# The opening of a two-layer hybrid backbone: order of the first loads, conditioning rows spread by TensorE, and narrow products of 128 columns

## What is computed

```
m_lat = silu(c)     @ ada_w[0] + ada_b[0]        # 9 x 1024 numbers: shift, scale, gate of three sub-layers
m_ctx = silu(c_ctx) @ ada_w[0] + ada_b[0]
h     = rms_norm(x, g) * (1 + scale) + shift     # the context tokens use m_ctx, the latent ones m_lat
x     = x + 0.5 * gate * (silu(h @ W_g) * (h @ W_u)) @ W_out
```

## Time and profile before

| | us |
|---|---|
| median of 3 runs | 2028.41 |
| lowest and highest of them | 2027.28, 2032.01 |
| the profiled execution | 2026.99 |
| its span | 2025.2 |
| PE busy in it | 1984.8 (98%) |
| DVE busy | 1282.0 (63%) |
| ACT busy | 752.2 (37%) |

### The profile page before, as it was taken

How to read it: one execution, slowest core, us unless ns; L and a number is a source line. 1 busy time by engine, 2 the same in 40 slices (tenths; PEclk the granted TensorE clock), 3 DMA queues, 4 the chain that set the end, 5 groups by cost and what they waited for, 6 DMA issues and landing times.

```text
span 2025.2 us, 27640 instructions
## 1 busy us (share of the span) xinstructions
PE 1984.8 (98%) x10255; PEld 1684.6 (83%) x10255; DVE 1282.0 (63%) x1840; ACT 752.2 (37%) x990; POOL 109.3 (5%) x165
## 2 busy tenths in 40 slices
PE   9999999999999999999999999999999999989998
PEld 7888888896788889888888988888887888878886
DVE  6877577775648776877677743453345632656666
ACT  5322222345545334332222342212235432736453
POOL 1010010000003200100001000000000000000000
PEclk8999999999999999999999999999999999999999
DMA  8455455521210003555555532352234422044553
GB/s 351 167 192 180 167 197 167 197 94 42 86 71 21 1 18 108 198 186 174 180 191 170 171 122 98 99 177 103 63 126 149 152 95 104 22 161 141 177 188 123
DMA packets 52650, 274.80 MB, mean 136 GB/s; under 512 B 6128, under 2 KB 7472, under 8 KB 34256
## 3 DMA queue, kind: packets, MB, share of 16 engines
q1 hardware_dynamic: 33024, 203.97, 29.1%
q0 software_dynamic: 18960, 68.88, 10.3%
q10 hardware_dynamic: 576, 0.69, 0.1%
HBM read 272.47 MB, written 1.05 MB: 135 GB/s over the span
## 4 chain that ended last, share of the span: by engine, by line
PE 92%; DVE 4%; ACT 3%; issue 1%; DMA 0%; DVEq 0%; ACTq 0%; SPq 0%
PE ps L1025 15%; PE ps L1027 15%; PE ps L1026 15%; PE ps L1037 8%; PE ps L1255 6%; PE ps L1256 6%; PE ps L1257 6%; PE ps L1038 4%; PE ps L2402 2%; PE ps L2404 2%; PE ps L2403 2%; PE ps L1907 1%; PE ps L1919 1%; PE ps L2488 1%; PE ps L1915 1%
## 5 line engine op out<-in xcount | busy, mean ns | idle before, releaser
L684 DVE TENSOR_TENSOR w_lo<-w_raw,w_hi 128x2048 fp32r<-128x2048 f32 (+3 forms) x206 | 420.8, 2043 | 194.3 <-ACT w_hi L463 193.8
L1025 PE MATMUL ps<-h_parts,w_lo 128*128 128x512 f32 (+1 forms) x1424 | 536.9, 377 | 1.5 <-DVE w_lo L684 0.6
L1027 PE MATMUL ps<-h_parts,w_hi 128*128 128x512 f32 (+1 forms) x1424 | 534.3, 375 | 0.0
L1026 PE MATMUL ps<-h_parts,w_hi 128*128 128x512 f32 (+1 forms) x1424 | 534.2, 375 | 0.0
L463 ACT ACTIVATE w_hi<-w_raw 128x2048 fp32r<-128x2048 f32 (+3 forms) x207 | 353.9, 1710 | 441.4 <-PE ps L1257 254.0
L692 DVE SCALAR_TENSOR_TENSOR ada_product<-ada_w,silu_c 128x1024 bf16<-128x1024 f32 x256 | 313.2, 1223 | 21.1 <-DVE ada_product L692 10.3
L1025 PEld LDWEIGHTS ps<-h_parts,w_lo 128*128 128x128 f32 x1424 | 268.4, 188 | 51.1 <-DVE h_parts L2240 1.1
L1027 PEld LDWEIGHTS ps<-h_parts,w_hi 128*128 128x128 f32 x1424 | 268.3, 188 | 48.5
L1026 PEld LDWEIGHTS ps<-h_parts,w_hi 128*128 128x128 f32 x1424 | 268.4, 189 | 47.5
L475 ACT ACTIVATE sil<-ps 128x512 f32<-128x512 f32 x66 | 39.5, 598 | 481.1 <-PE ps L1027 481.1
L1255 PE MATMUL ps<-hid_parts,w_lo 128*128 128x512 f32 x468 | 182.1, 389 | 0.0
(11 more groups left out here) (337 smaller groups left out, 2545.4 us busy)
## 6 DMA issues: line engine op xcount, KB each, us to landing
w_raw<-in_w_up SPq DMA_DIRECT2D x88, 1024.0 KB, 4.8
ada_w<-in_ada POOLq DMA_DIRECT2D x128, 512.0 KB, 3.6
w_raw<-in_w_down SPq DMA_DIRECT2D x32, 768.0 KB, 4.2
w_raw<-in_w_down SPq DMA_DIRECT2D x32, 640.0 KB, 3.9
w_raw<-in_w_ret_t SPq DMA_DIRECT2D x16, 1024.0 KB, 4.8
w_raw<-in_w_ab SPq DMA_DIRECT2D x14, 1024.0 KB, 4.8
ada<-in_ada SPq DMA_DIRECT2D x8, 1024.0 KB, 21.9
w_raw<-in_w_ret SPq DMA_DIRECT2D x8, 1024.0 KB, 4.8
```

Source lines behind the costliest of these rows:

```text
L684: dve.tensor_tensor(w_lo[parts_of(s, slot)][:, 0:elems], w_raw[slot][:, 0:elems], w_hi[parts_of(s, slot)][:, 0:elems].bitcast(F32), ALU.su ...
L1025: pe.matmul(out, lo, rhs_hi(k), start=first and k == 0, stop=False)
L1026: pe.matmul(out, hi, rhs_lo(k), start=False, stop=False)
L1027: mm = pe.matmul(out, hi, rhs_hi(k), start=False, stop=last and k == nk - 1)
```

## The change

Loads: `ada00[0]` is issued ahead of x. The two broadcast loads of the conditioning rows are gone from SP; ACT now issues them first of all its loads, as two rows of 1024 numbers into partition 0. ACT's order changes: Silu of `c_cols` and of the one-partition rows comes first, then the squares, then the table of the root. PE spreads the rows over the partitions with four products of one row by 512 columns, between the sums of squares; DVE copies the context half out of PSUM and ACT the latent half. The narrow products stream 128 columns (the pair of conditioning columns 64 times over) in place of 2. Both narrow products of chunk 0 run ahead of the sums, chunk 1 also gets its shift from a narrow product (TURNED = 2), and DVE's order of the first chunks is another. Of 49 dummy products in all, 18 stay.

```diff
     def sp_program(sp):
         sp.dma_start(c_cols, a["c_cols"]).then_inc(c_cols_loaded, 16)
+        scale_and_shift(0)
         for i in range(KD // 2):
             sp.dma_start(x[:, 2 * i:2 * i + 2], a["xT"][:, 2 * i:2 * i + 2]).then_inc(x_loaded[i], 16)
         weights(0)
-        scale_and_shift(0)
-        sp.dma_start(silu_c[:, 0, :], a["c_ctx"].partition_broadcast(P)).then_inc(c_loaded, 16)
-        sp.dma_start(silu_c[:, 1, :], a["c"][0, :].partition_broadcast(P)).then_inc(c_loaded, 16)
         scale_and_shift(1)
...
     def scalar_program(act):
+        for st, row in enumerate((a["c_ctx"].unsqueeze(0), a["c"])):
+            act.dma_start(silu_c[0:1, st, :], row).then_inc(c_loaded, 16)
...
-        act.wait_ge(sem("eps_set"), 1)
-        act.activation(warm_root[:], vecs[:, 2:3], ACT.Sqrt).then_inc(warmed, 1)
+        act.wait_ge(c_cols_loaded, 16)
+        act.activation(c_cols, c_cols, ACT.Silu).then_inc(c_silu, 1)
+        act.wait_ge(c_loaded, 32)
+        act.activation(silu_c[0:1], silu_c[0:1], ACT.Silu).then_inc(c_silu, 1)
         for r in range(0, KD, 2):
             act.wait_ge(x_loaded[r // 2], 16)
             act.activation(first_squares[:, r], x[:, r], ACT.Square).then_inc(even_squared, 1)
+        act.wait_ge(sem("eps_set"), 1)
+        act.activation(warm_root[:], vecs[:, 2:3], ACT.Sqrt).then_inc(warmed, 1)
         act_root(act, "n00", 0, 1.0 / D)
-        act.wait_ge(c_cols_loaded, 16)
-        act.activation(c_cols, c_cols, ACT.Silu).then_inc(c_silu, 1)
+        act.wait_ge(c_spread, 2)
+        act.activation(silu_c[:, 1, :].rearrange("p (b n) -> p b n", b=2), ps[:, 2:4, :], ACT.Copy).then_inc(c_spread_lat, 1)
         split_hi(act, 0, 0, ELEMS[0])
-        act.wait_ge(c_loaded, 32)
-        act.activation(silu_c[:], silu_c[:], ACT.Silu).then_inc(c_silu, 1)
         act_modulate(act, "n00")
...
+        dve.wait_ge(c_spread, 1)
+        dve.tensor_copy(silu_c[:, 0, :].rearrange("p (b n) -> p b n", b=2), ps[:, 0:2, :]).then_inc(c_spread_ctx, 1)
         dve_inverse(dve, "n00", 0)
...
         rows(0)
-        rows(1)
         split_lo(dve, 0, 0, ELEMS[0])
         low(0)
-        dve.wait_ge(c_silu, 2)
-        dots(1)
+        rows(1)
         split_lo(dve, 1, 1, ELEMS[1])
-        for c in range(2, KD):
-            if c > 2:
-                dots(c)
-            low(c - 1)
-            if c == 2:
-                dots(c)
-            rows(c)
+        rows(2)
+        dve.wait_ge(c_spread_ctx, 1)
+        dots(2, (0,))
+        low(1)
+        dve.wait_ge(c_spread_lat, 1)
+        dots(2, (1,))
+        for c in range(3, KD):
+            rows(c)
+            dots(c)
+            low(c - 1)
...
+    def pe_narrow(pe, n, w):
+        if w == 0:
+            pe.wait_ge(ada00_ready[n], 16)
+        for k in range(KD):
+            pair = c_cols[:, 2 * k:2 * k + 2].unsqueeze(1).to_broadcast([P, P // 2, 2])
+            mm = pe.matmul(ps[:, 5 + n % 2, w * P:(w + 1) * P].rearrange("p (r s) -> p r s", s=2),
+                           first_weights(n)[:, w, k * P:(k + 1) * P], pair, start=k == 0 and w == 0,
+                           stop=k == KD - 1, skip_group_check=True)
+        return mm
+
+    def pe_spread_c(pe, st, half):
+        return pe.matmul(ps[:, 2 * st + half, :], one_column[0:1, 0:1].to_broadcast([1, P]),
+                         silu_c[0:1, st, half * 512:(half + 1) * 512], start=True, stop=True)
...
-        pe.wait_ge(c_silu, 1)
-        pe.wait_ge(ada00_ready[0], 16)
-        narrow(0, 0)
-        idle(pe, 4)
-        narrow(0, 1).then_inc(scale_made, 1)
-        idle(pe, 4)
-        scale(1)
+        narrow(1, 0)
+        narrow(1, 1).then_inc(scale_made, 1)
         main(0, 0)
-        idle(pe, 4)
         scale(2)
-        idle(pe, 2)
         main(0, 1)
...
     def tensor_program(pe):
         pe.wait_ge(idle_set, 2)
-        idle(pe, 20)
+        idle(pe, 13)
+        pe.wait_ge(c_silu, 1)
+        pe_narrow(pe, 0, 0)
+        pe_narrow(pe, 0, 1).then_inc(scale_made, 1)
         for i in range(KD // 2):
             pe.wait_ge(pair_summed, i + 1)
...
             mm.then_inc(ssq_done, 1)
-            idle(pe, 3)
+            if i == 0:
+                pe.wait_ge(c_silu, 2)
+                pe_spread_c(pe, 0, 0)
+                pe_spread_c(pe, 0, 1).then_inc(c_spread, 1)
+            elif i == 1:
+                pe_spread_c(pe, 1, 0)
+                pe_spread_c(pe, 1, 1).then_inc(c_spread, 1)
+            elif i == 2:
+                idle(pe, 2)
+        idle(pe, 3)
         pe.wait_ge(const_loaded, 16)
         pe_rstd(pe, "n00", 0)
-        idle(pe, 3)
```

More of the change, by code:

```diff
@@ L375, in build @@
     scale_made, first_dot, first_mod = sem("scale_made"), sem("first_dot"), sem("first_mod")
+    c_spread, c_spread_ctx, c_spread_lat = sem("c_spread"), sem("c_spread_ctx"), sem("c_spread_lat")
+    TURNED = 2
     def sp_program(sp):
@@ L596, in one @@
                                scale=norm_g[:, 0, c:c + 1])
-                if c:
-                    act.wait_ge(first_dot, 2 * c)
-                act.activation(mod[:, 0, 1, :, c], mcol[:, :, c] if c else ps[:, 5, 2:4], ACT.Identity,
+                if c >= TURNED:
+                    act.wait_ge(first_dot, 2 * (c - TURNED + 1))
+                act.activation(mod[:, 0, 1, :, c], ps[:, 5 + c % 2, P:P + 2] if c < TURNED else mcol[:, :, c], ACT.Identity,
                                bias=mbias[:, c:c + 1]).then_inc(first_mod, 1)
@@ L939, in rows, with dots @@
             dve.tensor_tensor(prod[:, c % 2], x[:, c], ps[:, NRM, :], ALU.mult).then_inc(normed, 1)
-        def dots(c):
+        def dots(c, streams=range(2)):
             dve.wait_ge(ada00_ready[c], 16)
-            for st in range(2):
-                n = 2 * (c - 1) + st
+            for st in streams:
+                n = 2 * (c - TURNED) + st
                 if n:
@@ L1128, in idle @@
             pe.matmul(ps[:, 7, :], idle_tile[:, 0:P], idle_tile[:], start=True, stop=True)
+    def pe_narrow(pe, n, w):
[10 more added lines that the diff above has]
+                         silu_c[0:1, st, half * 512:(half + 1) * 512], start=True, stop=True)
     def pe_first_pairs(pe):
         def narrow(n, w):
[L1134 to L1138, removed]
+            return pe_narrow(pe, n, w)
         def scale(n):
-            pe.wait_ge(ada00_ready[n], 16)
-            if n >= 2:
-                pe.wait_ge(first_mod, n - 1)
+            pe.wait_ge(first_mod, n - 1)
             narrow(n, 0).then_inc(scale_made, 1)
@@ L1148, in main @@
                 pe_ready(pe, s)
+                pe.wait_ge((c_spread_ctx, c_spread_lat)[s], 1)
             pe.wait_ge(h_lo_done, k + 1)
@@ L2734, in lay_out @@
         "ada00": np.stack([columns(ada_w[0, :, D:2 * D], KD),
-                           np.concatenate([columns(ada_w[0, :, 0:D], KD)[:1],
-                                           ada_w[0, :, 0:D].T.reshape(KD, P, D)[1:]])], axis=2),
+                           np.concatenate([columns(ada_w[0, :, 0:D], KD)[:2],
+                                           ada_w[0, :, 0:D].T.reshape(KD, P, D)[2:]])], axis=2),
         "c_cols": np.stack([c_ctx.reshape(KD, P), c.reshape(KD, P)], axis=-1).transpose(1, 0, 2).reshape(P, 2 * KD),
```

## The result

| us | before | after |
|---|---|---|
| median of 12 runs | 2025.88 | 2030.26 |
| lowest, highest | 2024.25, 2032.01 | 2027.92, 2034.43 |
| the profiled execution | 2026.99 | 2027.95 |
| its span | 2025.2 | 2026.2 |

The ratio after to before is 1.0019 [1.0011, 1.0028]: the changed kernel is about 3.9 us slower. The forecast was 1.65 us faster. The size is near what a measurement can tell, but the interval excludes no change, so the sign was wrong. The median lies inside the stated range of 2022.3 to 2031.2 all the same: the range was wide, and its high end stood for no change with scatter and part of an early low clock.

What follows compares the result with a forecast made beforehand. PE was taken to bound the kernel (92% of the span in the chain of waits). Round 3 at 41.0 instead of 42.63 gave -1.65 us, other terms counted 0 or hidden: median 2028.41 to 2026.8, range 2022.3 to 2031.2.

Steps and rivals of the forecast that it cites:

- Landings: Opening loads: first weight tile lands at 8.2 us, x 1 MB later, w0 at 15.7, w1 at 20.6.
- PE up to the sums: PE's opening: two narrow calls 3.5, sums 3.2, spreads 3.6, dummies 0.45 us; sums end at 18.95, against 13.67.
- the low clock early: Rival: half clock from 8.2 us through the first spread pair, +6.1 on the path, +4.4 in sum; chance 0.07.
- Silu's table: First Silu of the FFN: its own table load, 1.28 us, hidden in 2.55 idle; behind the wait it adds 1.28.
- The page that was weighed: Skill pages: 1.38 us drain beside the table load, sum then -1.55; clock halved by idleness, so 128 columns win nothing.
- Up to round 3: DVE's chain, then PE's: round 1 at 31.3, round 2 at 36.4, round 3 at 41.0 for 42.63, -1.65 us.
- rounds and end: Later rounds: narrow call 1.75 for 1.68, counted 0 (bounds -0.5 and +1.3); DVE stays hidden, end as before.
- The copies out of PSUM: DVE and ACT copying the spread rows: done at 16 and 20.3 us, before `main` needs them; DVE's counted free.
- Clock not kept: Rival: half clock stays from about 20 to 30 us, round 2 at 38.0; 0.0 change, 2028.4 us; chance 0.12.
- slow columns: Rival, narrow calls: repeated columns stream at double time, 1.75 us more per call, 2037 us in all; chance 0.02.

Runs made afterwards that it cites:

- all_held: The changed kernel with sums streaming 128 columns, spreading products 128 rows high and Silu's table loaded early; 2023.96 us, ratio 0.9981 to before.
- two_columns: The changed kernel with its narrow products back at 2 columns; 2039.75 us, ratio 1.0058 to before.
- silu_table: The changed kernel plus a one-column Silu behind the first modulation's last use of ACT, to load the table early; 2029.66 us, ratio 1.0009 to before.
- combined: Before with wide narrow products and sums, chunk 1's shift by narrow product, fewer dummies, changed DVE order, modulation tiles 0 and 1 behind w0; 2025.56 us, ratio 0.9990.
- tile2_first: combined with the third modulation tile loaded ahead of the broadcast rows; 2024.82 us, ratio 0.9992 to before.
- wide_both: The kernel before with narrow products and sums both made 128 columns wide, nothing else; 2024.62 us, ratio 0.9988 to before.
- broadcast: The changed kernel with the rows loaded by two broadcast loads behind w0, no spreading products or copies, two dummies behind each of three sums; 2026.81 us, ratio 1.0000.
- second_spread_late: all_held with the second pair of spreads behind the last sum in place of five dummies, ACT's copy behind w0's high part; 2022.94 us, ratio 0.9979 to before.

## Why the prediction was wrong

**Landings: mis-sized, the good way.** The tile landed at 1.34 + 5.04 = 6.4, not at 8.2. I had taken the row of an x piece in the same stretch; the 4.8 of a tile alone was nearer. PE began the first narrow call at 6.51, so that is a gift of 1.7, which the next step lost.

**PE up to the sums: this step failed.** It priced every sum at 0.79 and every instruction of a spread at 0.45, the prices at full clock, and said "the work that was cheap there stood in for dummies". The terms were right where the clock was full: a pair of narrow calls 3.81 (3.5 forecast), the first sum 0.79, the first pair of spreads 1.91 (1.8). But one-column sums and one-row spreads are products behind which the clock falls, as two-column ones did in the earlier trace rows. I had read that in the row and then applied it to the narrow calls alone. From 15.1 on the later sums cost 1.80 and 1.50, and the sums ended at 20.69, not at 18.95 or, with the early landing, 17.25. From there to `rows(0)` it took 3.04 (23.73 - 20.69) in place of 1.82, at half clock too, and `main(0, 0)` came at 27.90, not at 25.2. all_held is the counter-proof: with the same order and the clock kept it came at 24.09, and the forecast, 25.2 less the early landing's 1.7, is 23.5. The order's arithmetic stood; its clock did not. The size of the failed term is 42.76 - 39.09 = 3.7 in the profile. In the medians it is 7.7 less the table's 2.0, so 5.7, and the forecast was off by 3.9 + 1.65 = 5.55.

**The rival that came true in part** is the low clock early (+4.4 forecast, +3.9 measured). It gave two reasons. The wait for the tile was to let the clock fall in the narrow calls; PE waited only 0.36 there, and the narrow calls, the first sum and the first spreads, which make up all of the +6.1, ran at 1.00. The other, that a product of one row may count as little, is what the runs bear out, together with the one-column sums, which it didn't suspect. The fall came behind the first spreads and cost what stands behind them. That the two sizes agree is luck: no term of the rival's sum came true.

**Silu's table: "Hidden" failed, its price was right.** The load stood behind the wait: in the chain of after it is 1.28 at 61.61, and two_columns shows it idle 2.52 for PE. The earlier trace rows at 803.45 misled: there the load ran ahead of the wait, and so it did in after at 804.41. In the program, that Silu has one wait ahead of it and the first Silu has two, one on loads and one on PE's step; that this is why the load stood behind PE's step is argued, as no run took one of them away. Loading the table early (silu_table) gave about 2.0 in the median; 1.28 lies within that measurement's error.

**The page that was weighed.** Of a drain of 1.38 beside the load (the Trainium skill, "ScalarE: Activation LUTs", section What ACT_TABLE_LOAD costs), the trace shows none: the Silu of two_columns starts at 73.49, and the load ended at 73.47. The rule of "TensorE: Matmul & The Clock Gate" (the Trainium skill), Part 1, that idleness halves the clock and activity frees it, is not what two_columns shows, with 34.10 us busy at half clock. combined and tile2_first agree with its first half: their clock fell behind or within waits of PE of 1.82 and 3.90. In this case both count, how long PE waits and what it is busy with.

**Up to round 3, rounds and end.** Round 1 was DVE's, as forecast: its `low(1)` came last, and PE waited 0.70 for it. From round 1 to 2 it is 4.84 (5.1 forecast, as DVE's chain) and PE's own work, from 2 to 3 4.74 (4.6), narrow calls 1.78 (1.75). The copies out of PSUM do not stand in the chain of after.

**Clock not kept, slow columns.** The first was priced at 0.0, with half clock at the old place; the place moved ahead with the cheap work. Slow columns are excluded by the 1.78 of a narrow call.

**Profile and median.** The profile of after explains +1.6 up to the first Silu, the median says +3.9. The 2.4 us between the profiles of after and silu_table, which have one order of PE, show that the fall's place varies and that after's profile was a mild one; that this makes up the 2.3 is argued, not shown. Why wide_both, combined and broadcast gain 2.6 to 3.2 us in their openings and 0 to 2.4 in the median stays open. The part behind the first Silu, which the change doesn't touch, took from 1960.2 us (wide_both) to 1967.9 (broadcast) in the fourteen profiles, a spread of 7.7 us, more than any opening gained or lost but that of two_columns. Stretches at half clock lie there too, near 513, 620, 688 and 1820 us in after; wide_both has none near 513 and 688. No run held this part apart, so a single profile shows the mechanism in the opening and not the price of a kernel.

## What to carry to other kernels

A product that uses few columns or few rows of the array is not filler for TensorE: before such work is moved ahead of the critical step, price it at half clock too, or make it 128 by 128, which cost 0.10 us a sum (1.05 for 0.95 in the timelines of all_held and after) and nothing a spread. Waits count as well: those of 1.82 and 3.90 us of PE in combined and tile2_first went with half clock. Where a table load is said to be hidden, look in the trace on which side of the wait it stands, and don't take it from another place of the same line; a one-column call of the function in an earlier idle place took 0.20 us and settles the matter. Move a load only together with the work that it feeds: the order of loads alone cost 5.9 us, 1.6 of it in the opening of its profile.

## What was not expected of the hardware

- A TensorE that is busy without a pause can stay at 1.2 GHz for 34.1 us (two_columns), and stay at 2.4 GHz for the whole opening when the same products are 128 wide and high (all_held).
- The fall is not fixed by the program: the same order of PE fell at 15.1 for 10.24 us in one execution (after) and at 13.3 for 13.65 in another (silu_table).
- A granted clock of 1.00 in a row does not mean full speed at the very start. In the chain of second_spread_late, thirteen dummies of 512 columns take 0.42 each, where the two at 16.68 in the chain of all_held are 0.43 together:

```profile
1.48 5.51 PE ps L1141 x13
```
- The first MB of weights, with only the 8 KB of `c_cols` issued ahead of it, landed 5.0 us after its issue, where the second half MB of x took 6.4.
